# Norms of two latents computed in the stage that makes them, keys and values in a new order of jobs, values in 2 KB rows

## What is computed

```python
proj = rmsnorm(x, g_pre) @ w_in            # 2048 tokens, D_MODEL 1024
(c_q, c_kv, k_pe, gate_a, hq, hf, hi, gate_b, merge_logits) = split(proj)   # c_q 768 wide, c_kv 256
q  = rmsnorm(c_q,  g_q)  @ w_uq            # 8 heads x (64 + 32)
kv = rmsnorm(c_kv, g_kv) @ w_ukv           # 8 heads x (64 key + 64 value)
# rotary part of q and of the key k_pe that all heads share
attn = chunk_causal_attention(q, k, v)     # mask by chunks of 64 tokens
y_a  = (attn * silu(gate_a)) @ w_branch_a
y_b  = (rmsnorm(hgrn2(hq, hf, hi)) * silu(gate_b)) @ w_branch_b
x = x + rmsnorm((gates_a * y_a + gates_b * y_b) @ w_out, g_post)
```

## Time and profile before

| | |
|---|---|
| median of 3 runs | 2369.13 us (2368.55 to 2373.09) |
| the profiled execution | 2375.12 us, span 2373.3 us, granted clock 0.972 |
| TensorE busy | 2220.7 us, 94% |
| VectorE, ScalarE, POOL busy | 1035.3, 907.4, 300.3 us |
| input projection | 0 to 700 us |
| merge logits and recurrence | 700 to 1206 us |
| latent projections | 1206 to 1441 us |
| attention, output | 1441 to 2373 us |

### The profile page before, as it was taken

The page is one execution under the profiler, slowest core; times in us unless marked ns, Lnnn a source line. Parts: engine busy times, 40 slices in busy tenths (PEclk is TensorE's granted clock), DMA queues, the critical chain, the costliest instruction groups (busy, mean ns, idle before and its releaser), DMA issues. The chain is left out here.

```text
span 2373.3 us, 33277 instructions
## 1 busy us (share of the span) xinstructions
PE 2220.7 (94%) x11664; PEld 1840.5 (78%) x11664; DVE 1035.3 (44%) x1864; ACT 907.4 (38%) x1683; POOL 300.3 (13%) x200
## 2 busy tenths in 40 slices
PE   6999999999979999999967899999999998899998
PEld 5888888778767888888856777788888786778886
DVE  6000000100004555554436746777777676565652
ACT  7111111000114444444335334666566565443441
POOL 1221224032201111111100000000000014200000
PEclk9999999999989999999978998999999999999999
DMA  5222222231212323333257654332123326574751
GB/s 178 85 68 75 75 75 76 80 106 57 94 61 76 97 88 97 97 93 97 71 200 223 197 178 118 69 72 58 40 49 72 72 79 197 171 221 123 219 151 66
DMA packets 213196, 256.41 MB, mean 108 GB/s; under 512 B 39360, under 2 KB 138048, under 8 KB 209600
## 3 DMA queue, kind: packets, MB, share of 16 engines
q1 hardware_dynamic: 188352, 208.21, 30.8%
q10 hardware_dynamic: 23616, 43.00, 4.8%
q0 software_dynamic: 1152, 4.19, 0.5%
HBM read 157.31 MB, written 98.04 MB: 108 GB/s over the span
## 5 line engine op out<-in xcount | busy, mean ns | idle before, releaser
L74 PE MATMUL bankD<-hT_hi,shared_w_hi 128*128 128x512 f32 x512 | 212.3, 415 | 11.7 <-POOLq L703 11.7
L74 PE MATMUL bankA<-hT_hi,shared_w_hi 128*128 128x512 f32 x544 | 212.7, 391 | 0.0
L76 PE MATMUL bankA<-hT_hi,shared_w_lo 128*128 128x512 f32 x544 | 211.9, 390 | 0.0
L75 PE MATMUL bankA<-hT_lo,shared_w_hi 128*128 128x512 f32 x544 | 211.9, 390 | 0.0
L76 PE MATMUL bankD<-hT_hi,shared_w_lo 128*128 128x512 f32 x512 | 201.7, 394 | 0.0
L75 PE MATMUL bankD<-hT_lo,shared_w_hi 128*128 128x512 f32 x512 | 201.0, 392 | 0.0
L1770 DVE TENSOR_REDUCE small_chunk_min<-scores 128x1 f32<-128x512 f32 (+2 forms) x320 | 181.0, 605 | 33.6 <-PE scores L76 18.9
L1790 ACT ACTIVATE probs<-scores,small_least 128x1024 f32<-128x1024 f32 (+2 forms) x192 | 167.3, 872 | 13.2 <-DVE small_least L1777 12.0
L74 PE MATMUL bankA<-wt_hi,hT_hi 128*128 128x512 f32 x384 | 152.6, 397 | 13.3 <-DVE shared_v_raw L392 7.7
L313 ACT ACTIVATE stage<-bankA 128x512 f32<-128x512 f32 x68 | 40.7, 598 | 301.6 <-PE bankA L76 300.1
L75 PE MATMUL bankA<-wt_lo,hT_hi 128*128 128x512 f32 x384 | 150.8, 393 | 0.0
(11 more groups left out here) (247 smaller groups left out, 4673.8 us busy)
## 6 DMA issues: line engine op xcount, KB each, us to landing
projT<-stage ACTq DMA_DIRECT2D x68, 256.0 KB, 2.4
shared_w_raw<-in_w_in_dram SPq DMA_DIRECT2D x32, 512.0 KB, 4.4
projT<-d_stage ACTq DMA_DIRECT2D x64, 256.0 KB, 2.4
e_l_in<-projT SPq DMA_DIRECT2D x64, 256.0 KB, 4.8
gateTok<-stage ACTq DMA_DIRECT2D x32, 256.0 KB, 2.0
shared_w_lo<-hgTok SPq DMA_DIRECT2D x16, 512.0 KB, 3.4
knT<-b_out SPq DMA_DIRECT2D x32, 256.0 KB, 2.9
vTok<-b_out SPq DMA_DIRECT2D x32, 256.0 KB, 3.7
```

Of the source, the lines that this page charges most:

```text
L74: pe.matmul(out, a_hi, b_hi, start=first, stop=False)
L75: pe.matmul(out, a_hi, b_lo, start=False, stop=False)
L76: return pe.matmul(out, a_lo, b_hi, start=False, stop=last)
```

## The change

- `input_projection`: while tiles 0 to 7 are copied out, ScalarE also squares each of their banks (`latent_square`; tiles 6 and 0 straight into `c_squares`, the others into `c_square`), and VectorE adds these. After tile 9 TensorE does all 32 sums over partitions (`latent_sums`), ScalarE two roots (`latent_roots`), VectorE reciprocals and the factor -SCALE for queries; after tile 11 TensorE transposes the factors (`latent_row`), and ScalarE writes them to HBM in two forms, `rsRow` (a row for each latent) and `rsTok` (by token). Tiles 10 to 13 stand outside TensorE's loop, and tiles 0 to 11 outside ScalarE's.
- `latent_projections`: squares, additions, sums, roots, reciprocals and spreads go. `load_c` also loads the factors of its block, spread over all partitions, into `rs`; `rsTok` is loaded once into `rstd`. Key, value and query blocks stay in their order; the jobs beside the evictions are placed anew, with all weight parts in KV blocks 0 and 1, and the latents of query block 1 prepared in KV block 3. `turned` has 5 buffers instead of 3.
- SP's order: the tables of block 0 go out at the start, those of the next block after the fourth output's store; latents go out at the head of a block, after all stores of the block before; the loads of query block 1's latents, of the shared key, its stores, and the first shared key for the attention are all placed later.
- `vTok` becomes [16, 128, 1024]: a value tile is stored in rows of 2 KB, and a head's values are read in pieces of 512 B.

```diff
+                def latent_sums():
+                    pe.wait_ge(const_set, 2)
+                    pe.wait_ge(c_sq_added, len(SUMMED) * NB)
+                    pe.wait_ge(bank_free, N_LORA * NB + (8 + B_NORM + 1))
+                    for g in range(2):
+                        for t in range(TT):
+                            last = pe.matmul(bank[:, B_NORM, g * TT + t:g * TT + t + 1], c_squares[:, g, t * P:(t + 1) * P], ones[:],
+                                             start=True, stop=True)
+                    last.then_inc(c_sums_done, 1)
+                latent_sums()
+                tile_products(0, N_LORA + 2, (c_std_ready, 2))
+                tile_products(1, N_LORA + 3)
+                latent_row()
+                tile_products(0, N_LORA + 4, (c_row_ready, 1))
...
+        for i in range(2):
+            beside(KV, 0, i, ("c", KV, 1, i))
+        for i in range(6):
+            beside(KV, 0, 2 + i, ("w", 2 * i), ("w", 2 * i + 1))
+        for i in range(3):
+            beside(KV, 1, i, ("w", 12 + 2 * i), ("w", 13 + 2 * i))
         for i in range(2):
+            beside(KV, 1, 3 + i, ("c", KV, 2, i))
+            beside(KV, 2, i, ("c", KV, 3, i))
+        for i in range(KQ):
+            beside(KV, 2, 2 + i, ("c", Q, 0, i))
+            beside(KV, 3, 1 + i, ("c", Q, 1, i))
+            for blk in (1, 2):
+                beside(Q, blk, i, ("c", Q, blk + 1, i))
...
+                sp.dma_start(rs[:, g, blk % 2], rsRow[g:g + 1, block_cols(blk)].to_broadcast([P, BLK])).then_inc(c_in[blk % 2][g], 16)
+
+            def load_c_again(blk, g):
+
+                sp.wait_ge(prod_done, products_of(g, blk - 2))
+                if g == Q:
+                    sp.wait_ge(cs_ready, (blk - 2) * 2 + 2)
+                load_c(blk, g)
...
+                        dma = sp.dma_start(vTok[blk * TPB + i - V_AT, :, part * BLK:(part + 1) * BLK], src)
...
-                    if g == KV and i == KV_EV - 2 and blk + 2 < NB:
-                        sp.wait_ge(prod_done, number(KV, blk + 1, 0))
-                        load_c(blk + 2, KV)
-                    if g == Q and i == X_AT and blk + 2 < NB:
-                        sp.wait_ge(prod_done, number(Q, blk + 1, 0))
-                        load_c(blk + 2, Q)
+                    if g == KV and blk in (1, 2) and i == 0:
+                        load_c_again(blk + 1, KV)
+                    if (g, blk, i) == (KV, 2, 2):
+                        load_c(1, Q)
+                    if g == Q and blk in (1, 2) and i == 0:
+                        load_c_again(blk + 1, Q)
                     store(g, blk, i)
-                    if (g, blk, i) == (Q, 0, 2):
+                    if (g, blk, i) == (KV, 3, 2):
+                        load_k()
+                    if (g, blk, i) == (Q, 0, 3):
                         store_k(0)
+                    if (g, blk, i) == (Q, 1, 3):
+                        store_k(1)
+                    if g == Q and blk + 1 < NB and i == X_AT - 1:
+                        sp.wait_ge(cs_ready, blk * 2 + 2)
+                        load_cs(blk + 1)
...
-                    if (g, blk, i) == (Q, 1, X_AT):
+                    if (g, blk, i) == (Q, 2, X_AT):
                         sp.wait_ge(k_stored, 16 * 4 * NB)
                         attend.load_first_shared_key(sp)
...
-            act.wait_ge(const_in, 48)
+            act.wait_ge(const_in, 64)
...
                 sp.dma_start(v_sb[u][:].bitcast(F32),
-                             vTok[ds(i * 2 + u, 1)].rearrange("o p t n -> (o p) t n")).then_inc(head_in[u], 16)
+                             vTok[:, :, ds(i * (2 * P) + u * P, P)].rearrange("t p n -> p t n")).then_inc(head_in[u], 16)
```

More of the change, by code:

```diff
@@ L148, in input_projection @@
         lb_exp = sem("lb_exp")
+        c_sq_ready = sem("c_sq_ready")
+        c_sq_added = sem("c_sq_added")
+        c_sums_done = sem("c_sums_done")
+        c_std_ready = sem("c_std_ready")
+        c_rstd_step = sem("c_rstd_step")
+        c_row_turned = sem("c_row_turned")
+        c_row_ready = sem("c_row_ready")
+        c_stored = sem("c_stored")
+        FIRST_OF_NORM = (KQ, 0)
+        SUMMED = [n for n in range(N_LORA) if n not in FIRST_OF_NORM]
+        B_NORM = NB - 1
         N_TILES = T_PE + 1
@@ L319, in _ @@
                     act.sem_inc(s, 16)
-                with act.Fori(0, T_HF // 2) as i:
-                    for u in range(2):
-                        tile_out(i * 2 + u, u, ACT.Copy)
+                for n in range(N_LORA + 2):
+                    tile_out(n, n % 2, ACT.Copy)
+                latent_roots()
+                for n in range(N_LORA + 2, T_HF):
+                    tile_out(n, n % 2, ACT.Copy)
+                latent_rows_out()
                 with act.Fori(0, (T_PE - T_HF) // 2) as i:
@@ L373, in _ @@
                             lo_half(g - 1, half)
+                for n in SUMMED:
+                    g = int(n < KQ)
+                    for blk in range(NB):
+                        m, cols = SUMMED.index(n) * NB + blk, slice(blk * BLK, (blk + 1) * BLK)
+                        dve.wait_ge(c_sq_ready, n * NB + blk + 1)
+                        if m >= NB:
+                            dve.wait_ge(c_sq_added, m - NB + 1)
+                        dve.tensor_tensor(c_squares[:, g, cols], c_squares[:, g, cols], c_square[:, m % 2], ALU.add)\
+                           .then_inc(c_sq_added, 1)
+                dve.wait_ge(c_std_ready, 2)
+                dve.reciprocal(c_rstd[:], c_std[:]).then_inc(c_rstd_step, 1)
+                dve.wait_ge(c_rstd_step, 1)
+                dve.tensor_scalar(c_rstd[:, TT:2 * TT], c_rstd[:, TT:2 * TT], -SCALE, None, ALU.mult).then_inc(c_rstd_step, 1)
                 lb_in, lb_tmp, lb, span = shared.lb_in, shared.lb_tmp, shared.lb, shared.span
@@ L434, in tile_products @@
                         pe.wait_ge(bank_free, n * NB + (blk + 1))
+                        if norm_read is not None and blk == B_NORM:
+                            pe.wait_ge(*norm_read)
                         cols = slice(blk * BLK, (blk + 1) * BLK)
@@ L441, in _ @@
                 tile_products(1, 1)
-                with pe.Fori(1, T_PE // 2) as i:
+                with pe.Fori(1, N_LORA // 2 + 1) as i:
+                    for u in range(2):
+                        tile_products(u, i * 2 + u)
+                latent_sums()
[3 more added lines that the diff above has]
+                tile_products(0, N_LORA + 4, (c_row_ready, 1))
+                tile_products(1, N_LORA + 5)
+                with pe.Fori(N_LORA // 2 + 3, T_PE // 2) as i:
                     for u in range(2):
@@ L1036, in latent_projections @@
     KV, Q = 0, 1
[L1037 to L1038 removed]
+    BLOCKS = tuple((g, blk) for g in (KV, Q) for blk in range(NB))
+    EVICTIONS, TURNS = (KV_EV, Q_EV), (PAIRS, Q_EV)
+    NUMBERS = [(g, blk, i) for g, blk in BLOCKS for i in range(EVICTIONS[g])]
+    TURN_USES = [(g, blk, i) for g, blk in BLOCKS for i in range(TURNS[g])]
     TILES = (tuple(range(KQ, N_LORA)), tuple(range(KQ)))
@@ L2488, in hybrid_mla_hgrn2_gated_merge @@
         small = Small(nc, ctx)
-        latent_sems, latent = latent_projections(nc, small, projT, g_q, g_kv, w_uq, w_ukv, rope, ident, qnT, qpT, knT, kpT, vTok)
+        latent_sems, latent = latent_projections(nc, small, projT, rsRow, rsTok, g_q, g_kv, w_uq, w_ukv, rope, ident, qnT, qpT, knT, kpT, vTok)
         attend_sems, attend = attention(nc, small, latent, qnT, qpT, knT, kpT, vTok, ident, oA)
```

259 lines of the change are left out of this document (79 added, 180 removed).

## The result

The changed kernel took **2393.27 us** (4 runs, 2389.59 to 2396.19), where the kernel before took 2369.56 beside it: a ratio of 1.0099, 95% interval 1.0084 to 1.0114, slower by 23.7 us. The forecast was 2364 us, faster by 5.2, with a range up to 2378: wrong in sign and outside the range.

What follows compares the result with a forecast made beforehand. TensorE was taken to bound the input projection, VectorE the keys and values, and latents late in SP's queue the queries. The terms +7.5 + 0 - 12.7 + 0 gave -5.2 us, so 2364 us, range 2347 to 2378.

Steps and rivals of the forecast that it cites:

- Sums: Input projection: 32 one-column matmuls and the transpose on TensorE lengthen the kernel by 7.5 us, all on the path.
- a partly lowered clock, 0.7: Input projection: 0.7 us added to the 6.5 us of one-column matmuls for a clock below the upper level.
- rival 5: Input projection: the sums stall it at half clock, +7 us more, 2371 us, no change; chance 0.07.
- Keys and values: Latent stage: VectorE sets the pace; queries start at 1284.1 where it was 1303.8, a gain of 19.7 us.
- rival 3: Key stage: half clock for keys and values, 82 us instead of 63.6, 2382 us; chance 0.08.
- Block 2: Queries: latents issued late behind small SP issues, so query block 2 starts 42.0 us after block 1; before, 35.5.
- (e): Query block 3: same queue, latents issued at +8, landed at +16.5, start 33.5 us after block 2; before, 33.1.
- Last block: Last query block: 42.3 us before, spread gone (-0.9), shared key for first scores loaded later (+1.5, 0 to 6).
- Attention: Attention proper: values read in 512 B pieces, even a doubled load hides; cost 0 us (-0.5 to +1).
- Carrying the 6 us over: Whole time: profiled execution was 6.0 us above the median of 2369.1, in no stage read; the change was carried over.
- signs of being right: Sums of 7 us, queries after about 64, TensorE idle over 10 before query block 2, its latents issued over 10 late.
- Rival 2: Query blocks: latents of blocks 2 and 3 land late, 14 us each, twice +6, 2376 us, slower; chance 0.16.

Runs made afterwards that it cites:

- the experiment that keeps the clock: The changed kernel with the 32 one-column sums put two by two behind groups of three dense matmuls in the next tile: 2385.6 us, 1.0060.
- the kernel before with few issues: The kernel before the change with the small transfers of shared key and tables merged into fewer issues, nothing else: 2371.53 us beside 2371.54, 0.9995.
- the kernel with three edits: The changed kernel with latents of query blocks 2 and 3 loaded sooner, sums between dense matmuls, values laid out as before: 2361.2 us, 0.9961.
- five mends less the one of `vTok`: The changed kernel with query latents sooner, sums between dense matmuls, few issues, roundings paired beside outputs 1 to 3, values in 2 KB rows: 2359.53 us, 0.9951.

## Why the prediction was wrong, step by step

The miss is 19.8 us, and three steps make 19.0 of it: the issue of block 3's latents taken over from block 2 (8.5), the load left out beside the value stores (5.7), and the clock in the sums (4.8). No single one decides: with the largest put right the span would still be 6 us longer than before.

- **Sums: +7.5 forecast, +12.3 measured.** The count and the upper-clock price were right (7.4 us for the sums, 7.9 to the stage's first product, in the experiment that keeps the clock). The step that failed is "a partly lowered clock, 0.7". In the block of 32 the granted clock was 0.64, the block took 10.93 us, and dense matmuls followed 0.43 us apart for 5.7 us. That is rival 5, which was given 0.07.
- **Start of the latent stage: 0 forecast.** SP's first latent load moved by 12.4 us and TensorE's first product by 12.3: right.
- **Keys and values: 63.6 us forecast, 69.3 measured.** The pace of blocks 0 and 1 was right (VectorE's scaling for block 2 begins at 1270.06; 1257.5 + 12.3 = 1269.8 by the forecast), and so was ScalarE's added wait for the latents of block 3 (5.6 forecast, 6.0 measured). The step that failed is that block 2's values would keep to VectorE's pace: left out was the 1.75 MB load of query latents that the change puts beside the value stores, and one slot waited 4.4 us behind it. Moving the load to key block 3 gives 63.2 us to this mark, but puts its waits into that block. "Halve SP's issue time" did not come out either: the eight value stores of key block 3 took SP 4.7 us, 6.5 before.
- **Clock in the key stage.** The Trainium skill, TensorE: Matmul & The Clock Gate, section "A second HAM failure mode: psum-queue depth-cycling", says that short idles between groups of matmuls waiting for PSUM banks can make the clock swing, which spoke for rival 3. By the rows rival 3 did not come: the granted clock was 0.87, higher than the 0.83 before. In the changed kernel waits for banks of 0.7 to 1.6 us left it up; products ran 0.43 us apart behind the 7.48 us without work ahead of 1266.61, and for 3.3 us behind the 4.00 us wait for a bank ahead of 1294.89. Before, they did so behind waits of 2.5 to 5.0 us for `b_acc`.
- **Block 2: 42.0 us after block 1 forecast, 43.5 measured.** The mechanism was as written: the load behind 24 small issues (15.6 us after block 0's products, 13.7 forecast), 8.4 to land (8 forecast), a chain of 19.5 (19.3 forecast). The working holds a slip of 1 us: 1323.3, 8 and 19.3 add up to 1350.6, not 1351.6. And the row at 1329.98 is that of sums of squares; block 1's first product before came at 1330.79, so block 1 to block 2 was 34.5 us there.
- **Block 3: 33.5 us forecast, 42.0 measured.** This is the largest miss, 8.5 us, and the step that failed is (e), "for block 3 the same queue: issued at +8". The issue came 15.6 us after block 2 began, 7.6 us of the miss; landing (9.3) and chain (17.0) make the rest. The second half of the shared key's stores and another 16 table loads stand there as well, 11.1 us of SP. SP reaches them only behind the stores of block 1's outputs, which wait in the chain of block 2's latents (1362.36 for the third). On top comes the 5 us in which SP stands behind the 512 B reads. The forecast saw these reads only as transfers hidden in attention.
- **Last block: 42.9 forecast, 45.4 measured**, of which 3.4 is the scores' wait for the shared key (+1.5 forecast, with a bound of 6).
- **Attention: 0 forecast.** 930.3 us against 932.5. The layout makes no difference there that can be seen. But this stretch, whose work is that of the kernel before in both of the following, took 928.2 us in the kernel before with few issues and 934.3 us in the kernel with three edits:

```profile
1440.70:2368.90 928.20, 873.23 (x4679) 733.03 (x4679) 606.93 (x1126) 493.05 (x948) 48.73 (x34) 0.98 0.41 112
```

```profile
1430.90:2365.20 934.30, 875.66 (x4679) 734.82 (x4679) 605.05 (x1126) 493.74 (x948) 49.03 (x34) 0.98 0.41 112
```

The misses add up: 4.8 + 5.7 - 1.0 + 1.5 + 8.5 + 2.5 - 2.2 = 19.8 us, so -5.2 becomes +14.6, and the two spans differ by 14.5. The medians differ by 20 to 24 us. The profiled execution of the kernel before lay 6 us above its median, and that of the changed kernel 3.7 below; 6 us of scatter in one stretch can make this difference, and no row places it. The two other profiles that lay 5 to 6 us above their kernel's median, that with three edits and that with five mends less the one of `vTok`, are also those with the longest such stretches (934.3 and 934.7 us). Carrying the 6 us over was sound only as long as both profiles stood alike to their medians.

The sum's structure held. Its largest step, a gain of 20 us in the key stage, was only 14; but a later load of the query latents, which brings the first query product where the forecast had it, makes the kernel no faster, since block 2 waits for latents that SP issues when it did. The queue of SP weighed most: putting the two loads ahead of the small issues brings back the whole loss. The forecast followed this queue for the latents of one block with care and then gave the next an old number.

The forecast's signs of being right nearly all came: an idle stretch of over 10 us ahead of block 2 ended by `b_c_lo`, ScalarE released by the landing, an issue over 10 us after block 0's products. They tested block 2, where the forecast was right, and none tested block 3. Rival 2 is nearest in time (2376, slower), but not in cause: the two loads landed in 8.4 and 9.3 us, not in 14.

## What to carry to other kernels

Write out the issuing queue for every repetition of a loop that it passes through, not for the first one alone: a load that waits for its buffer should stand directly behind what frees it, ahead of small transfers that nobody needs yet, and small transfers should be merged where one access pattern covers them. Here either is worth 20 to 25 us of 2393, and in an order that doesn't put the load behind them, nothing. Many narrow matmuls in a row are better put between wide ones, a few at a time (4.7 us here). A wait that disappears at one mark has to be looked for behind it before it is called a gain. And a stage that is made faster passes its gain on only if the next stage's start doesn't hang on something else.

## What the runs showed of the hardware

- A block of 32 one-column matmuls, with TensorE busy throughout, took the granted clock to 0.64, and matmuls of 512 columns behind it ran 0.43 us apart for 5.7 us; in groups of two between dense matmuls it stayed at 1.00.
- A read of 1 MB in 512 B pieces (values of one head from rows of all heads) was followed by a pair of issues that took the same queue 5.4 to 6.7 us in each of the eleven profiles that have it. Behind a read in whole rows by head the pair took 0.9 to 1.2 us, in six profiles.
- 16 issues of a 32 KB load took SP 7.4 to 9.7 us; the same table in 2 issues with a broadcast source took 1.3 to 2.9 us.
